# Hymba-style decoder step on one core: the two extra expert blocks joined by a matrix of shared rows, and the first expert blocks' rows turned between halves of products

## The reference, cut to what matters

```
x = x + concat([y_a, y_b]) @ w_out
combine = weights of the two chosen experts of each row, 0 elsewhere      # 32 experts
for e in range(32):
    he  = silu(h2 @ w_gate[e]) * (h2 @ w_up[e])
    out = out + combine[:, e:e+1] * (he @ w_down[e])
x = x + out
y = rmsnorm(x, norm_final)
```

## Time and profile before

| | |
|---|---|
| median of 3 runs | 993.68 us (992.49 to 997.74) |
| profiled execution | 992.78 us, span 991.0 us |
| TensorE products busy | 948.0 us, 96% of the span |
| DVE / ScalarE / GpSimd busy | 691.9 / 490.7 / 190.5 us |
| mean granted TensorE clock | 0.984 |

### The profile page before, as it was taken

One profiled execution on the slowest core, in us unless ns is written; L12 is line 12 of the kernel. 1 busy time (PEld: TensorE's weight loads), 2 busy tenths in 40 slices (PEclk: granted clock), 3 DMA queues, 4 the chain that ended last, 5 costly groups with the idle time before them and its releaser, 6 DMA issues.

```text
span 991.0 us, 14779 instructions
## 1 busy us (share of the span) xinstructions
PE 948.0 (96%) x5400; PEld 820.3 (83%) x5400; DVE 691.9 (70%) x1037; ACT 490.7 (50%) x890; POOL 190.5 (19%) x154
## 2 busy tenths in 40 slices
PE   5999999998999999999999998899999999999991
PEld 4889999998999999999888887577777777777750
DVE  7467767689453544636656666779999999999873
ACT  7578777432422232223323222256666666665872
POOL 2000000000000000000030001324546464555214
PEclk9999999999999999999899999999999999999996
DMA  7104676523755644556623226999999999999991
GB/s 250 51 25 141 164 176 140 168 88 119 228 146 150 158 137 118 156 142 202 229 102 128 94 82 256 328 416 413 415 415 414 412 404 409 396 415 413 391 360 59
DMA packets 123643, 230.66 MB, mean 233 GB/s; under 512 B 71660, under 2 KB 84518, under 8 KB 114878
## 3 DMA queue, kind: packets, MB, share of 16 engines
q1 hardware_dynamic: 108102, 202.69, 59.0%
q0 software_dynamic: 15408, 26.97, 7.3%
q10 hardware_dynamic: 72, 0.20, 0.0%
HBM read 205.33 MB, written 53.63 MB: 261 GB/s over the span
## 4 chain that ended last, share of the span: by engine, by line
PE 81%; DVE 9%; DMA 4%; ACT 4%; issue 2%; SPq 0%; POOL 0%; POOLq 0%; DVEq 0%; ACTq 0%
PE psum L1150 25%; PE psum L2321 12%; PE psum L2067 10%; PE psum L2411 8%; PE psum L2325 5%; PE psum L2259 3%; DVE xi L956 2%; DVE it L954 2%; PE psum L1173 1%; PE psum L2002 1%; PE psum L1255 1%; DVE acc L898 1%; PE psum L1242 1%; PE psum L1248 1%; PE psum L1259 1%
## 5 line engine op out<-in xcount | busy, mean ns | idle before, releaser
L1150 PE MATMUL psum<-hh,wh 128*128 128x350 f32 x672 | 223.3, 332 | 2.7 <-issue 2.7
L1150 PE MATMUL psum<-hh,wl 128*128 128x350 f32 x672 | 217.9, 324 | 0.0
L1150 PE MATMUL psum<-hl,wh 128*128 128x350 f32 x672 | 217.3, 323 | 0.0
L1150 PEld LDWEIGHTS psum<-hh,wh 128*128 128x128 f32 x672 | 127.7, 190 | 4.0 <-issue 2.9
L1150 PEld LDWEIGHTS psum<-hl,wh 128*128 128x128 f32 x672 | 127.4, 190 | 0.9
L1150 PEld LDWEIGHTS psum<-hh,wl 128*128 128x128 f32 x672 | 127.2, 189 | 0.0
L2297 DVE TENSOR_TENSOR wgu_lo<-wgu,wgu_hi 128x1536 fp32r<-128x1536 f32 x60 | 105.4, 1759 | 17.7 <-ACT wgu_hi L2292 17.7
L2292 ACT ACTIVATE wgu_hi<-wgu 128x1536 fp32r<-128x1536 f32 x60 | 89.2, 1488 | 1.6 <-DMA new_ssm_sample<-s_in 1.6
L2321 PE MATMUL psum<-wgu_hi,xgt_hi 128*128 128x512 f32 x180 | 85.6, 475 | 0.0
L1694 POOL IOTA r_iw<- 128x8 f32 x1 | 0.1, 142 | 413.1 <-DMA mixer_rows<-th 413.1
L856 DVE TENSOR_TENSOR wl<-wst,wh 128x1024 fp32r<-128x1024 f32 x28 | 34.3, 1225 | 60.6 <-ACT wh L630 60.5
(11 more groups left out here) (352 smaller groups left out, 1882.4 us busy)
## 6 DMA issues: line engine op xcount, KB each, us to landing
wgu<-w_gate SPq DMA_DIRECT2D x34, 1024.0 KB
wgu<-w_up SPq DMA_DIRECT2D x34, 1024.0 KB
wd<-w_down SPq DMA_DIRECT2D x34, 1024.0 KB
wst<-w_in SPq DMA_DIRECT2D x28, 512.0 KB, 4.1
ck<-qkv_rows SPq DMA_DIRECT2D x9, 702.0 KB
qkv_rows<-acc SPq DMA_DIRECT2D x12, 520.0 KB, 6.1
xb<-x SPq DMA_DIRECT2D x8, 512.0 KB, 4.2
wo<-w_out SPq DMA_DIRECT2D x8, 512.0 KB, 6.8
```

The costliest lines, as they stand in the source:

```text
L1150: ins = mm(ps[:, c, 0:ZC], w[:, kk, :], a[:, kk, c * ZC:(c + 1) * ZC], start=(kk == 0 and q == 0), stop=(kk == KD - 1 and q == 2))
```

## The change

In the start, TensorE's order is written out anew: half of block 0's gate and up products, turn of block 1, the other half, half of block 1's products, turn of block 2, turn of block 0's gated rows, the other half, the table products, down of block 0. Then the steps begin with j = 1. ScalarE copies block 1's turned rows before block 0's `tanh`.

In the end, blocks 32 and 33 no longer pass sums through memory. While the early blocks run, TensorE and DVE make `shared`, a 128 x 128 matrix with 1 where a slot of block 32 and a slot of block 33 hold the same row, and `first_y_rows`, block 32's row numbers with those of shared rows put out of bounds. DVE keeps 32's weighted output apart in `first_part` (`add_first`). TensorE multiplies `shared` by it (`cross`) and DVE adds the product to 33's sums (`join`). GpSimd gathers the sums for both blocks together, the scatter of 32's sums stays only for more than two extra blocks, and the last two sends go out without a wait between them. The norms and scales of blocks 30 and 31 stand before block 33's sigmoid.

```diff
+    def diagonal(dve):
+        nc.vector.tensor_scalar(second_diag[:, :], b.ident[0:C, 0:C], b.extra_rows_f[:, 1:2], None, ALU.mult
+                                ).then_inc(diag_ok.sem, 1)
+        nc.vector.tensor_copy(first_rows[:, :], b.extra_rows_f[:, 0:1]).then_inc(diag_ok.sem, 1)
+
+    def list_second(pe):
+        pe.wait_ge(diag_ok.sem, diag_ok.at(2))
+        pe.wait_ge(main[0].sum_ok.sem, main[0].sum_ok.at(1))
+        nc.tensor.matmul(ps[0:C, 4, 0:C], b.ones[0:C, 0:C], second_diag[:, :], start=True, stop=True
+                         ).then_inc(listed.sem, 1)
+
+    def compare(dve):
+        dve.wait_ge(listed.sem, listed.at(1))
+        nc.vector.tensor_scalar(shared[:, :], ps[0:C, 4, 0:C], first_rows[:, 0:1], None, ALU.is_equal
+                                ).then_inc(shared_ok.sem, 1)
+        dve.wait_ge(shared_ok.sem, shared_ok.at(1))
+        nc.vector.tensor_reduce(first_only[:, :], shared[:, :], AX.X, ALU.add).then_inc(shared_ok.sem, 1)
...
+    def add_first(dve, x):
+        dve.wait_ge(x.q.down_ok.sem, x.q.down_ok.at(x.n + 1))
+        nc.vector.tensor_scalar(first_part[:, :].rearrange("c (h d) -> c h d", h=2), ps[0:C, 4:6, :], weight(x.id), None,
+                                ALU.mult).then_inc(joined.sem, 1)
+        dve.wait_ge(x.q.sum_in.sem, x.q.sum_in.at(16 * (x.n + 1)))
...
+        nc.vector.tensor_tensor(total[0][:, :], first_part[:, :], before[0][:, :], ALU.add).then_inc(x.q.sum_ok.sem, 1)
+
+    def cross(pe):
+        pe.wait_ge(joined.sem, joined.at(1))
+        for c in range(2):
+            nc.tensor.matmul(ps[0:C, 4 + c, :], shared[:, :], first_part[:, c * 512:c * 512 + 512], start=True, stop=True
+                             ).then_inc(crossed.sem, 1)
+
+    def join(dve, x):
+        dve.wait_ge(x.q.sum_ok.sem, x.q.sum_ok.at(x.n + 1))
+        for c in range(2):
+            dve.wait_ge(crossed.sem, crossed.at(c + 1))
+            half_ = total[1][:, c * 512:c * 512 + 512]
+            nc.vector.tensor_tensor(half_, half_, ps[0:C, 4 + c, :], ALU.add).then_inc(joined.sem, 1)
...
@@ gpsimd
-            gather_sum(pool, main[0], 0, NE)
-            scatter_sum(pool, main[0], 0, 16, NE)
+            for p in range(2):
+                gather_sum(pool, main[p], p, NE + p)
             final.stored(pool)
-            for j in (28, 29):
-                send_rows(pool, j - LATE, normed[j - LATE], block_of(j).id)
-            pool.wait_ge(main[0].sum_out.sem, main[0].sum_out.at(16 * STEPS))
-            gather_sum(pool, main[1], 1, NE + 1)
-            for j in (30, 31):
+            for j in range(28, 32):
                 send_rows(pool, j - LATE, normed[j - LATE], block_of(j).id)
             count = extra_blocks(pool)
+            pool.wait_ge(y_sent.sem, y_sent.at(16 * 4))
             for k in range(2):
-                pool.wait_ge(y_sent.sem, y_sent.at(16 * (4 + k)))
                 send_rows(pool, 4 + k, normed[4 + k], NE + k)
             with pool.If_lt(pool.to_reg(2), count):
                 pool.wait_ge(y_sent.sem, y_sent.at(16 * 6))
+                scatter_sum(pool, main[0], 0, 16, NE)
+                pool.wait_ge(main[0].sum_out.sem, main[0].sum_out.at(16 * STEPS))
...
@@ scalar: norm_late(30) and norm_late(31) from half(33), behind copy_gated, to mid(33), before sigmoid
                 if isinstance(x.e, int) and x.e == 33:
+                    act.wait_ge(joined.sem, joined.at(3))
                     norm_late(x.e)
...
@@ vector, back
-                add_rows(dve, x.q, x.p, x.n, x.id, rows)
                 if isinstance(x.e, int) and x.e == 32:
-                    scale_late(30)
-                    scale_late(31)
+                    add_first(dve, x)
+                else:
+                    add_rows(dve, x.q, x.p, x.n, x.id, rows)
+                if isinstance(x.e, int) and x.e == 1:
+                    compare(dve)
+                if isinstance(x.e, int) and x.e == 33:
+                    join(dve, x)
                     scale_late(32)
-                if isinstance(x.e, int) and x.e == 33:
                     scale_late(33)
...
@@ tensor
+            def begin():
+                one, two, three = (block_of(j) for j in range(3))
+                front_(one)
+                sample.multiplied(pe)
+                pe.wait_ge(b.gu_landed[one.k], 32)
+                gate_up(pe, one.q, one.p, one.n, one.k, range(0, KD // 2))
+                front_(two)
+                gate_up(pe, one.q, one.p, one.n, one.k, range(KD // 2, KD))
+                pe.wait_ge(b.gu_landed[two.k], 32)
+                gate_up(pe, two.q, two.p, two.n, two.k, range(0, KD // 2))
+                front_(three)
+                half(one)
+                gate_up(pe, two.q, two.p, two.n, two.k, range(KD // 2, KD))
+                route.tensor_extra(pe)
+                back(one)
```

More of the change, by code:

```diff
@@ L2202, in expert_stage @@
     y_sent = Again(b.gathered[2], 16 * (NE // SLOTS))
+    shared = m.place("shared", [C, C], at=b.rw_at)
+    second_diag = m.place("second_diag", [C, C], at=b.rw_at + 512)
+    first_rows = m.place("first_rows", [C, 1], at=b.rw_at + 1024)
+    first_only = m.place("first_only", [C, 1], at=b.rw_at + 1056)
+    first_y_rows = m.place("first_y_rows", [C, 1], I32, at=b.rw_at + 1088)
+    first_part = normed[5]
+    diag_ok, listed, shared_ok, joined, crossed = (
+        s.again("x_diag"), s.again("x_listed"), s.again("x_shared"), s.again("x_joined"), s.again("x_crossed"))
     names = "turned xt_ok gu_ok tanh_ok ge_ok he_ok he_turned he_copied down_ok sum_ok".split()
@@ L2224, in send_rows @@
     def send_rows(pool, i, buffer, e):
         pool.wait_ge(late_ok.sem, late_ok.at(i + 1))
-        pool.indirect_dma_start(io.y, rows_of(e), buffer[:, :], None, bounds_check=TOK - 1, oob_is_err=False
+        rows = rows_of(e)
+        if isinstance(e, int) and e == NE:
+            pool.wait_ge(shared_ok.sem, shared_ok.at(4))
+            rows = bass.IndirectOffsetOnAxis(ap=first_y_rows[:, 0:1].bitcast(U32), axis=0)
+        pool.indirect_dma_start(io.y, rows, buffer[:, :], None, bounds_check=TOK - 1, oob_is_err=False
@@ L2301, in gate_up_bank, with gate_up @@
         return ps[0:C, p, :].rearrange("c (g f) -> c g f", g=2)
-    def gate_up(pe, q, p, n, k):
-        pe.wait_ge(q.xt_ok.sem, q.xt_ok.at(2 * n + 2))
-        for kk in range(KD):
+    def gate_up(pe, q, p, n, k, part=range(KD)):
+        if part[0] == 0:
+            pe.wait_ge(q.xt_ok.sem, q.xt_ok.at(2 * n + 2))
+        for kk in part:
             ins = nc.tensor.matmul(gate_up_bank(p), xt_f[p][:, kk, :], b.slots[k][0][:, :, kk, :],
                                    start=(kk == 0), stop=(kk == KD - 1))
-        ins.then_inc(q.gu_ok.sem, 1)
+        if part[-1] == KD - 1:
+            ins.then_inc(q.gu_ok.sem, 1)
     def gate_up_in_parts(pe, x):
@@ L2435, in block_of, with staggered @@
         return x
-    def staggered(eng, front, half, early, mid, late, back):
+    def staggered(eng, front, half, early, mid, late, back, begin, first=0):
         def step(j, i=0):
@@ L2445, in step @@
             back(block_of(j, i))
[L2447 to L2450, removed]
+        begin()
+        for j in range(first, 4):
             step(j)
@@ L2654, in mid @@
                     final.norms(act, (7, 8))
+                    norm_late(30)
+                    norm_late(31)
                 if isinstance(x.e, int) and x.e >= 30:
@@ L2673, in back @@
                 if isinstance(x.e, int) and x.e == 33:
+                    act.wait_ge(joined.sem, joined.at(3))
                     norm_late(x.e)
-            staggered(act, front_, half, early, mid, lambda y: gate_up_high(act, y, 1), back)
+            def begin():
+                front_(block_of(0))
+                front_(block_of(1))
+                mid(block_of(0))
+            staggered(act, front_, half, early, mid, lambda y: gate_up_high(act, y, 1), back, begin)
             def body(n):
@@ L2727, in mid @@
                     final.scales(dve, (6, 7, 8))
+                    scale_late(30)
+                    scale_late(31)
                 if isinstance(x.e, int) and x.e >= 30:
@@ L2735, in mid @@
                     route.vector_tables(dve)
+                    diagonal(dve)
                     gate_up_low(dve, block_of(PLAIN), 0)
@@ L2789, in back @@
                     pe.wait_ge(b.extra_ok.sem, b.extra_ok.at(1))
+                if isinstance(x.e, int) and x.e == 2:
+                    pe.wait_ge(shared_ok.sem, shared_ok.at(1))
                 if x.parts:
@@ L2794, in back, with begin @@
                     down(pe, x.q, x.p, x.n, x.k)
+                if isinstance(x.e, int) and x.e == 1:
+                    list_second(pe)
+                if isinstance(x.e, int) and x.e == 33:
+                    cross(pe)
+            def begin():
+                one, two, three = (block_of(j) for j in range(3))
[12 more added lines that the diff above has]
+                back(one)
             stages.tensor(pe)
             route.tensor(pe)
```

(2 more changed lines are left out.)

21 lines of the change are left out of this document (14 added, 7 removed).

## The result

Six executions of the changed kernel have a median of 984.48 us (983.03 to 986.03), six of the kernel before, on the same chip, 993.12 us. The ratio is 0.9878, with a 95% interval of 0.9832 to 0.9924. Applied to the 993.68 us from which the prediction started, this is 981.6 us (977.0 to 986.1), so it lies 1.4 us under the low end of the forecast range, 983.0. The ratio given is the middle of its interval. It isn't the ratio of the two medians, 0.9913, because two of the six executions of before took 997.74 and 1004.25 us; by its median, 984.48 us, the changed kernel lies inside the range. The same kernel was timed a second time later (experiment 7): 986.9 us, ratio 0.9954 [0.9924, 0.9984], which applied to 993.68 us is 989.1 us. Both intervals exclude 1; they meet only at 0.9924.

The account below looks back on a forecast made before the run. TensorE and DMA both full over 655 to 900 us, then a latency chain on GpSimd's queue. Span 984.2 (tail 6.8 less, start nothing) plus 1.78 is 986.0, or 986.9 against the median; forecast 986.5 us, range 983 to 989.8.

Parts of the forecast that it names:

- The tail: GpSimd's chain at the end: two gathers, six sends, one wait; span ends at 984.2 us, 6.8 us less.
- The prediction's last step: Send of block 33 starts at 979.6 to 980.8 us, with 3.96 us from its start to the end.
- The held send: Send 28 on GpSimd is held by DVE's add and ends 0.9 us after it, at 971.3 us.
- Rival (b): Further sends on GpSimd stretch under DVE's adds and scales, 3.2 to 4 us more; 989.5 us, chance 0.18.
- The start: Start of the expert stage: reordering removes TensorE's 1.18 and 1.43 us waits, but gains nothing in the total.
- the lead: TensorE's 2.3 us head start from the new order, expected to be lost waiting for the partial sums' landing.
- Rival (a): The start's gain comes through: GpSimd's chain starts at 964.3 us, a time near 984.2 us, chance 0.12.
- the same floor: Near the end, ScalarE waits for the first partial-sums tile, at 940.25 us before, however early TensorE is.
- Rival (c): TensorE's granted clock falls to half level in the reordered start, giving about 1013 us; chance 0.04.

Follow-up runs that it names:

- experiment 7: The changed kernel itself, unaltered, timed again on the same chip against the kernel before: 986.9 us, ratio 0.9954.
- start only: New start order with the old tail, on the kernel before: 990.61 us, ratio 0.9955.
- filled: Kernel before, order unchanged, with nine idle products put in TensorE's two pauses in the start: 989.87 us, ratio 0.9958.
- experiment 2: The changed kernel with its new start taken out, so new tail with old start: 987.17 us, ratio 0.9928.
- experiment 1: The kernel before with the new start order alone, tail untouched: 990.61 us against 992.67, ratio 0.9955.
- tail only: The changed kernel without its new start: 987.17 us against 992.67 for the kernel before, ratio 0.9928.

## Why the prediction was right in the tail and wrong in the start

**The tail** held nearly term by term. In us after the start of the gather for block 32: second gather 1.34 (forecast 1.33), first send 2.65 to 4.48 (2.63 to 4.66), second 4.78 (4.96), third 6.08 (6.26), fourth 7.35 (7.56), fifth 13.19, and 11.65 in the repeated run (11.7 to 12.9), end 17.8 and 16.0 (17.0 to 18.2). Over five profiles with the new tail and no wait put back this stretch is 17.8, 16.0, 15.9, 16.0 and 18.0 us, in before, start only and filled 24.4, 23.6 and 23.1: by the means 7.0 us less, for 6.8 forecast; by the medians of experiment 2 it is 5.5. The prediction's last step was off in two places that partly cancel: it let the last send come 1.3 us after the one before it and end 3.96 us after its start, as before. The first held (1.28), the second was 3.1 to 3.3 us. The baseline was long too, as one execution can be: in before the first send took 2.06 us, in the other seven profiles with the old tail 0.98. In start only it began 0.3 us ahead of the scaling that held it in before.

```profile
973.09 0.98 POOL L2226 DMA_INDIRECT y<-normed,slot_rows  x1 [0.30 <-issue]
...
973.39 1.28 DVE L2241 SCALAR_TENSOR_TENSOR normed<-total,late_stat,wn 128x1024 f32<-128x1024 f32 x1 [0.28 <-ACT late_stat L2236]
```

**The held send** was read rightly. In five of six profiles the first send lay under DVE's add with two inputs in SBUF and took 1.83 to 2.00 us; in the sixth, where the add began only 0.04 us ahead of it, 1.01. So overlap alone doesn't decide; these rows fit that the send is held where DVE's operation began ahead of it by more than that (0.11 us at least in the five). The Trainium skill, SBUF — State Buffer, section Who interferes with whom, infers that such an operation wouldn't hold descriptor generation; for these sends, which also read their row numbers (`slot_rows`) from SBUF, the rows disagree with it. Rival (b), more sends stretched, came in part: one further send of 1.49 and 1.63 us with 1.2 us of late landing in two profiles, nothing in three others.

**The start** is where it failed. The step is the last one of that part: "I expect the lead to be paid back here, and no gain from the start in the total". Its mechanism is there (idle ScalarE ahead of `y`; 5.8 us coming through once DMA is relieved, which is more than the 2.3 us of lead), but the step took one execution's balance for the kernel's. In the earlier trace rows TensorE's pauses cost 2.6 us and nothing more, and in the earlier trace rows TensorE and the DMA arrived within 0.34 us of each other. In the five other profiles with the old start's order TensorE came 1.0 to 3.6 us later than that, in four of them with 3.4 or 6.8 us at half clock after the pauses. The new start wins a part of that back, not all: four of the eight profiles with it have a half-clock stretch too, each after a pause of 0.7 to 1.7 us ahead of block 0's products, which the new order leaves. The missing term is about 2 us (2.1 by medians in experiment 1, interval 1.3 to 7.6 us by the ratio; 4.5 by medians from filling the pauses alone, on another chip). With it, 986.5 would have been 984.5, still above the 981.6 of the first measurement. The rest, some 3 us, no experiment explains; 984.5 lies within that measurement's interval, 977.0 to 986.1, and the second measurement, 989.1, lies above the forecast. So on which side of the range's low end the result fell was, as far as the runs tell, chance.

**Rival (a)**, 984.2 us, had the time but not the reason: it needed room in the DMA engines. What came, as far as the profiles show, was less work time on TensorE, up to the same floor. **Rival (c)** looked at the clock only as a danger of the new start. The old one had it, and the sentence against (c), that the new start has fewer pauses, was the argument for a gain.

The first measurement's 8.6 us by medians were a little more than the kernel's usual gain: the second gave 4.7. Between them lies the sum of the parts: 2.1 from start only and 5.5 from tail only, 7.6 us. Why single executions take such a stretch and others not, after the same pauses, stays open.

## What to carry to other kernels

A pause of TensorE isn't worth its own length only: where its granted clock can fall afterwards, look at several executions before costing it, and try idle products in it. Here they were an edit of a few lines. One profile in which two resources arrive within a fraction of a microsecond of each other says nothing on which of them usually sets the time; count both from a common event in several profiles. Passing partial results through a small matrix product instead of memory took a scatter and its landing out of this tail, and the gain could be worked out from GpSimd's timeline: 6.8 us, where profiles gave 7.0 and medians 5.5. Before taking one execution's tail as the baseline, see whether it holds a send that others don't.

## What the runs showed of the hardware

Pauses of 0.7 to 2.2 us on TensorE, in a stretch otherwise full, were followed before 655.5 us by the half clock level for 3.4 us or more at a time in 8 of 10 profiles, each stretch making products 1.1 to 2.4 us longer (8.15 for 7.03 us, and 9.43 over a stretch of 6.8 us; 5.38 for 3.68); with pauses of 0.3 us and less, in none of 4. One of these four, start only, had it later, at 945 to 948.7 us, behind a pause of 3.8 us. The mean granted clock of an execution goes with its time: 992.23 us at 0.986 to 0.988, 990.70 at 0.989 to 0.991. A send held under DVE took 1.5 to 2.0 us instead of 1.0, and in the two profiles where the fourth send was so held (1.49 and 1.63 us) the four sends also landed later: the wait behind it was 4.4 and 4.3 us instead of 3.1.
